# One stage of a two-block transformer kernel: the last two steps of a layer norm move to GpSimd, and three queues are reordered around them

## The chip, the cores and the metric

The kernel is one program on one core of a Trainium2 chip. The engines are TensorE (PE in the rows: matrix products and transposes; PEld: its weight loads), VectorE (DVE), ScalarE (ACT), GpSimd (POOL) and SyncE (SP), which here only issues DMAs. Each has a queue of its own, which it works in order; they meet at semaphores. The metric is the time of one execution on the device, in microseconds, as a median over runs; lower is better.

## The reference, cut to what matters

The program computes two transformer blocks on 2048 tokens of width 1024 in float32. The second block ends in a mixture of experts. The part that the change touches is what lies between attention and experts:

```
o   = concat(rmsnorm(o_mla), rmsnorm(o_gqa))           # halves of 512
h1  = layer_norm(ALPHA * h0 + o @ w_o, ln1_g, ln1_b)   # 1024 wide
logits = h1 @ w_router + b_router                      # 32 experts
top 4 experts and their softmax gates for each token
tables: for each expert the list of its tokens, then h1 gathered by expert
layer_norm(x, g, b) = (x - mean) / sqrt(var + 1e-5) * g + b
```

The experts then read h1 from DRAM (`h1d`), and their sums are added into a second copy (`sumd`).

## The kernel before, in words

The program is a chain of seven stages with a meeting of all engines between them: the mixer of the first block, its output product and norms (the *join* stage, tiles `j_...`), projections, attention, the *route* stage (tiles `o_...`), the experts (`e_...`), and a closing norm (`c_...`). The change is in the route stage alone, from about 2680 to 2975 us of the span.

The route stage works in 16 blocks of 128 tokens. Its loops run over i = 0 to 17, and each engine has an order of its own, written out by hand in `route_pe`, `route_act`, `route_dve`, `route_pool` and `route_sync`. The lists `b`, `a`, `v` and (after the change) `g` in `route_stage` repeat these orders; they give the semaphore values and the PSUM bank of each product (a ring of eight banks). No scheduler takes part.

In turn i the work is this.

- TensorE (`route_pe`): first half of the output product of block i (`project(i, 0)`, 24 matmuls, L2012), eight transposes of the attention output of block i+1 (`turn_o`, L1999), second half of the product (`project(i, 1)`); in its middle eight transposes of h1 of block i-1 (`turn_h`, L2021). Then the count of tokens per expert for block i-2 (`count`, L2035 and L2036) and the router product of block i-1 (`router`, L2028), which waits until ScalarE has copied the transposed h1 out of PSUM.
- ScalarE (`route_act`): rounds the transposed attention output (L2086), copies the transposed h1 into `hT` (L2103), takes the root of block i's variance (`lsd`, L2106), then the squares and the root for the RMS norm of block i+2 (L2077, L2079), then the exponentials of block i-1 (L2112). Roots and exponentials need different tables; a load of a table (ACT_TABLE_LOAD) stands between them.
- VectorE (`route_dve`): residual sum of each half (`residual`, L2149), low parts of the attention output (L2141), statistics of block i (`spread`, L2154 to L2156), `place(i-2)` (L2170 to L2176: where each token of block i-2 goes in the expert tables), `norm(i)` (L2161, and two products over 128x1024, L2165 and L2166, that give h1), `norms(i+2)` (the RMS norm of the attention output of block i+2: L2131, and L2134 twice), and `choose(i-1)` (L2181 to L2194: the top four experts of block i-1).
- GpSimd (`route_pool`): after loading constants, four scattering DMAs for each block (L2289) once `place` has written its slots. After the last it fetches the first table and gathers the first rows for the experts.
- SyncE (`route_sync`): loads of `od` and `h0d`, and for each block two stores of h1 once it is finished.

"T" is used below for the moment at which TensorE ends `project(i, 1)` and goes on to `count(i-2)`, the start of row L2035.

Of the kernel before, what the change touches and what calls it, by code (L numbers as in the profile page):

```python
# [1863 lines left out]
def route_stage(nc, A, banks, h0d, od, h1d, sumd, tabd, R, W, ident, eps_ln, eps_rms, since, ctx):  # L1864
# [25 lines left out]
    P.idf = sb("idf", [128, 16, 4])  # L1890
    sb("even", [128, 96])
    P.oTh = sb("oTh", [128, 2, 8, 128], F32R)
# [30 lines left out]
    for i in range(18):  # L1923
        now, nxt, back, far = i < 16, i + 1 < 16, 1 <= i < 17, i >= 2
        b += [("pj", i, 0)] if now else []
        b += [("to", i + 1, 0), ("to", i + 1, 1)] if nxt else []
        b += [("pj", i, 1)] if now else []
        b += [("th", i - 1, 0), ("th", i - 1, 1)] if back else []
        b += [("C", i - 2)] if far else []
        b += [("lg", i - 1)] if back else []  # L1930
        a += [("toh", i + 1, 0), ("toh", i + 1, 1)] if nxt else []
        a += [("th", i - 1, 0), ("th", i - 1, 1)] if back else []
        a += [("lsd", i)] if now else []
        a += [("sq", i + 2, 0), ("sq", i + 2, 1), ("sd", i + 2)] if i + 2 < 16 else []
        a += [("exp", i - 1)] if back else []
        v += [("pj", i, 0)] if now else []
        v += [("to", i + 1, 0), ("to", i + 1, 1)] if nxt else []
        v += [("pj", i, 1), ("st0", i), ("st1", i), ("ag", i)] if now else []
        v += [("C", i - 2), ("Macc", i - 2), ("pr", i - 2), ("pos", i - 2), ("sf", i - 2), ("slot", i - 2)] if far else []
        v += [("rs", i), ("ts", i), ("add", i)] if now else []  # L1940
        v += [("rms", i + 2), ("o", i + 2, 0), ("o", i + 2, 1)] if i + 2 < 16 else []
        v += [(n, i - 1) for n in ("lg", "m8", "i8", "idf", "ex", "neg", "oh", "M", "rec", "gate")] if back else []
    b += [("cnt",), ("tab",)]
    v += [("end", k) for k in range(34)]
# [9 lines left out]
def route_sync(nc, P):  # L1954
# [16 lines left out]
    for i in range(16):  # L1971
        if i + 2 < 16:
            load(i + 2)
        if i == 4:
            sp.wait_ge(*v.at("wo", 7))
            for c in range(2):
                sp.dma_start(P.R.raw[:, c].rearrange("p k n -> p (k n)"), A["wgu"][0, c]).then_inc(P.R.raw_full[c], 16)
        sp.wait_ge(*v.at("add", i))
        for d in (P.h1d, P.sumd):
            sp.dma_start(d[i * 128:(i + 1) * 128, :], P.h1[:, i % 3]).then_inc(*P.h1st[i % 3].more())  # L1980
# [4 lines left out]
def route_pe(nc, P):  # L1985
# [16 lines left out]
    def project(i, n):  # L2002
        p, f = opened("pj", i, n)
        if n == 0:
            pe.wait_ge(*v.at("to", i, 1))
        for k in range(8):
            if n == 1 and k == 4 and i >= 1:
                turn_h(i - 1)
            if i == 0 and n == 0:
                pe.wait_ge(*v.at("wo", k))  # L2010
            for m, (x, y) in enumerate(((P.oTh, P.woh), (P.oTh, P.wol), (P.oTl, P.woh))):
                t = pe.matmul(p[:, :], x[:, i % 2, k, :], y[:, k, n * 512:(n + 1) * 512],  # L2012
                              start=(k == 0 and m == 0), stop=(k == 7 and m == 2))
        t.then_inc(f, 1)

    def turn_h(i):
        pe.wait_ge(*v.at("add", i))
        for hf in range(2):
# [3 lines left out]
            t.then_inc(f, 1)  # L2022

    def router(i):
        p, f = opened("lg", i)
# [13 lines left out]
    for i in range(18):  # L2039
# [4 lines left out]
        if i < 16:  # L2044
            project(i, 1)
        if i == 16:
            turn_h(i - 1)
        if i >= 2:
# [66 lines left out]
def route_dve(nc, P):  # L2115
# [34 lines left out]

    def spread(i):
        x, s = P.hb[:, i % 3], P.sl_
# [3 lines left out]
        dve.bn_aggr(s[:, 12:14], s[:, 0:12]).then_inc(*v.step("ag", i))  # L2156

    def norm(i):
        x, y, s = P.hb[:, i % 3], P.h1[:, i % 3], P.sl_
        dve.wait_ge(*a.at("lsd", i))  # L2160
        link(dve.reciprocal(s[:, 15:16], s[:, 14:15]), "rs", i)  # L2161
        if i >= 3:
            dve.wait_ge(P.h1st[i % 3].sem, 32 * (i // 3))
            dve.wait_ge(*filled(P, ("th", i - 3, 1)))
        link(dve.scalar_tensor_tensor(out=y, in0=x, scalar=s[:, 12:13], in1=P.LN[:, 0, :], op0=ALU.subtract, op1=ALU.mult), "ts", i)  # L2165
        dve.scalar_tensor_tensor(out=y, in0=y, scalar=s[:, 15:16], in1=P.LN[:, 1, :], op0=ALU.mult, op1=ALU.add).then_inc(*v.step("add", i))  # L2166

# [46 lines left out]
    for i in range(18):  # L2214
# [4 lines left out]
        if i < 16:  # L2219
            residual(i, 1)  # L2220
            spread(i)
        if i >= 2:
            place(i - 2)
        if i < 16:
            norm(i)
        if i + 2 < 16:
            norms(i + 2)
        if 1 <= i < 17:
            choose(i - 1)
# [43 lines left out]
def route_pool(nc, P):  # L2273
# [10 lines left out]
    pool.wait_ge(P.const.sem, P.const.n)  # L2284
    pool.wait_ge(P.tab0.sem, P.tab0.n)
    for i in range(16):
        pool.wait_ge(*v.at("slot", i))
        for k in range(4):
            pool.indirect_dma_start(out=P.tabd, out_offset=bass.IndirectOffsetOnAxis(ap=P.slot[:, i, k:k + 1], axis=0),  # L2289
                                    in_=P.pair[:, i, k, :], in_offset=None).then_inc(*P.scat.more())  # L2290
    pool.wait_ge(P.scat.sem, P.scat.n)
# [849 lines left out]
```

## Time and profile before

| | us |
|---|---|
| median of 3 runs (lowest, highest) | 5685.53 (5682.82, 5690.87) |
| the profiled execution: its own time | 5690.87 |
| its span | 5689.7 |
| TensorE busy in the span | 5349.9 (94%) |
| VectorE busy | 3580.1 (63%) |
| ScalarE busy | 2682.3 (47%) |
| GpSimd busy | 744.9 (13%) |

The span is the time between the first and the last recorded instruction; the execution's own time is 1.2 us longer. The page of the profile gives the whole program; the route stage is about 5% of it, so it is read by windows and timelines. In a row of the timeline, a bracket says how long the engine was idle before the instruction and what it was waiting for; "issue" is a gap with no releaser in the records. Rows of several like instructions in succession are merged (x8), and the duration is from the first start to the last end.

### The profile page before, as it was taken

How to read it: one execution, taken by the hardware profiler on the slowest of the kernel's cores; microseconds unless marked ns; L12 is line 12 of the kernel's file. 1: busy time of each engine (PE TensorE's matmuls, PEld its weight loads, DVE VectorE, ACT ScalarE, POOL GpSimd, SP SyncE). 2: the span in 40 equal slices, each digit the busy share in tenths (PEclk: the TensorE clock that was granted, in tenths of full speed). 3: DMA queues.
4: the chain of work that ended last, by engine and by line, in shares of the span. 5: the costliest groups of instructions: out<-in, count | busy, mean ns of one | idle time of the engine just before them, and what ended most of it. 6: DMA issues, size and time to landing. Idle time of an engine off the chain costs nothing. (4 is left out here: it accounts for less than half of the span.)

```text
span 5689.7 us, 92463 instructions
## 1 busy us (share of the span) xinstructions
PE 5349.9 (94%) x30192; PEld 4771.6 (84%) x30193; DVE 3580.1 (63%) x6815; ACT 2682.3 (47%) x5312; POOL 744.9 (13%) x579
## 2 busy tenths in 40 slices
PE   8999979789799999998979999999999999999993
PEld 7777768678699999998768999999898888888883
DVE  6667757433466667776664755655667745477777
ACT  3444321333355556665333634543546534366664
POOL 1101125333100000000220100110101101010103
PEclk9999989899899999999989999999999999999997
DMA  3333234344510111201633744554557635477666
GB/s 142 115 115 101 92 124 167 113 130 138 171 59 28 39 53 38 74 33 51 161 105 114 249 151 153 197 169 155 194 188 234 232 127 169 136 230 247 240 226 229
DMA packets 260437, 809.25 MB, mean 142 GB/s; under 512 B 22304, under 2 KB 168448, under 8 KB 224512
## 3 DMA queue, kind: packets, MB, share of 16 engines
q1 hardware_dynamic: 230352, 717.05, 36.5%
q0 software_dynamic: 27536, 84.88, 6.8%
q10 hardware_dynamic: 2336, 4.45, 0.2%
q8 instruction: 136, 2.23, 0.2%
q14 instruction: 77, 0.63, 0.0%
HBM read 662.84 MB, written 143.47 MB: 142 GB/s over the span
## 5 line engine op out<-in xcount | busy, mean ns | idle before, releaser
L2726 DVE TENSOR_TENSOR e_wl<-r_raw,e_wh 128x1024 fp32r<-128x1024 f32 x770 | 930.6, 1223 | 480.0 <-DVEq L2354 479.3
L2575 PE MATMUL ps<-e_hT,e_wl 128*128 128x192 f32 (+5 forms) x4096 | 1196.6, 292 | 0.0
L2642 ACT CAST e_wh<-r_raw 128x1024 fp32r (+1 forms) x770 | 790.5, 1043 | 848.7 <-ACTq L2354 815.8
L2568 PE MATMUL ps<-e_hT,e_wh 128*128 128x384 f32 (+2 forms) x2560 | 797.6, 374 | 20.7 <-PEq L2354 20.3
L2575 PEld LDWEIGHTS ps<-e_hT,e_wl 128*128 128x128 f32 x4096 | 776.3, 190 | 10.7
L2570 PE MATMUL ps<-e_hT,e_wh 128*128 128x352 f32 (+2 forms) x1536 | 529.2, 345 | 9.0 <-PEq L2354 9.0
L2568 PEld LDWEIGHTS ps<-e_hT,e_wh 128*128 128x128 f32 x2560 | 480.4, 188 | 67.3 <-issue 27.2
L2574 PE MATMUL ps<-e_hT,e_wh 128*128 128x352 f32 (+2 forms) x1536 | 527.2, 343 | 0.0
L2596 PE MATMUL ps<-e_wh,e_aTh 128*128 128x512 f32 x1248 | 504.4, 404 | 5.0 <-PEq L2354 4.7
L1788 ACT CAST a_PT<-ps 128x512 fp32r<-128x512 f32 x512 | 288.0, 588 | 467.7 <-PE ps L1728 467.7
L1743 PE MATMUL ps<-a_PT,a_V 128*128 128x256 f32 (+1 forms) x3264 | 504.4, 294 | 0.2 <-DVE a_PT L1828 0.2
L1828 DVE TENSOR_TENSOR a_PT<-ps,a_PT 128x512 fp32r<-128x512 f32 (+1 forms) x640 | 377.6, 607 | 175.9 <-ACT a_PT L1788 158.4
L2596 PE MATMUL ps<-e_wh,e_aTl 128*128 128x512 f32 x1248 | 487.9, 391 | 0.0
L2596 PE MATMUL ps<-e_wl,e_aTh 128*128 128x512 f32 x1248 | 486.2, 390 | 0.0
L1815 DVE TENSOR_REDUCE a_sc<-ps 128x1 f32<-128x416 f32 (+1 forms) x640 | 365.1, 588 | 158.1 <-PE ps L1720 130.3
L1720 PE MATMUL ps<-a_K,a_Q 128*128 128x416 f32 (+1 forms) x1920 | 437.3, 358 | 17.5 <-DMA a_KR<-kTd 14.4
L1743 PEld LDWEIGHTS ps<-a_PT,a_V 128*128 128x128 f32 (+1 forms) x3264 | 419.4, 189 | 14.9 <-issue 13.5
L1800 ACT ACTIVATE a_P<-ps,a_sc 128x416 f32<-128x416 f32 (+1 forms) x640 | 386.2, 604 | 0.0
L1720 PEld LDWEIGHTS ps<-a_K,a_Q 128*128 128x128 f32 x1920 | 352.9, 190 | 30.9 <-issue 14.8
L386 PE MATMUL ps<-m_xh,m_wh 128*128 128x512 f32 x896 | 353.7, 395 | 5.3 <-DVE m_wl L671 5.3
L386 PE MATMUL ps<-m_xl,m_wh 128*128 128x512 f32 x896 | 349.7, 390 | 0.0
L386 PE MATMUL ps<-m_xh,m_wl 128*128 128x512 f32 x896 | 349.6, 390 | 0.0
(367 smaller groups left out, 9550.4 us busy)
## 6 DMA issues: line engine op xcount, KB each, us to landing
r_raw<-in_wgu SPq DMA_DIRECT2D x130, 2048.0 KB
r_raw<-in_wdn SPq DMA_DIRECT2D x64, 2048.0 KB
m_raw<-in_w SPq DMA_DIRECT2D x56, 1024.0 KB, 4.9
qTd<-p_qt SPq DMA_DIRECT2D x32, 640.0 KB, 6.6
e_bd<-in_bdn SPq DMA_DIRECT2D x32, 512.0 KB, 3.8
kTd<-p_kt SPq DMA_DIRECT2D x32, 448.0 KB, 3.7
a_Q<-qTd SPq DMA_DIRECT2D x7, 2048.0 KB, 9.4
a_V<-vd SPq DMA_DIRECT2D x24, 512.0 KB, 4.2
```

Of the source, the lines that this page charges most:

```text
L386: t = pe.matmul(p[:, :], x[:, w, i, j * 128:(j + 1) * 128], y[:, c % 2, i, :], start=(n == 0), stop=(n == 23))
L1720: t = pe.matmul(p[:, 0:w], x, y, start=(n == 0), stop=(n == len(todo) - 1))
L1743: t = pe.matmul(ps[b][:, 256 * half:256 * half + 256], P.V[0:r, j, x, :], P.PT[0:r, G % 2, y, j, :], start=(j == k == 0), stop=(j == NT - ...
L1800: act.activation(P.P[:, n % 2, lo:lo + w], p[:, 0:w], ACT.Exp, bias=P.sc[:, n % 2, 6:7], scale=SQK_M if P.steps[n][0] < 4 else SQK_G, accu ...
L1828: dve.tensor_tensor(lo, src, hi.bitcast(F32), ALU.subtract).then_inc(*v.step("t", n, c))
L2568: t = pe.matmul(both, wh, E.hT[:, :, k, 0:v], start=(k == 0), stop=False)
L2570: t = pe.matmul(p[:, 0:v], wh, E.hT[:, 0, k, 0:v], start=(k == 0), stop=False)
L2574: pe.matmul(p[:, 0:v], wh, E.hT[:, 1, k, 0:v], start=False, stop=False)
L2575: t = pe.matmul(p[:, 0:v], wl, E.hT[:, 0, k, 0:v], start=False, stop=(k == 7))
L2596: t = pe.matmul(E.G[g][:, :], x[:, 4 * h + k, b * 128:(b + 1) * 128], y[:, h, k * 512:(k + 1) * 512], start=(h == k == m == 0), stop=(h == ...
L2642: act.copy(E.wh[:, h, x], raw[:, 2048 * h + 1024 * i:2048 * h + 1024 * i + 1024]).then_inc(E.hi_full, 1)
L2726: return dve.tensor_tensor(lo, src, hi.bitcast(F32), ALU.subtract)
```

## The change

Four things are done in the route stage.

1. The layer norm of block i on VectorE is now one instruction, `tensor_scalar` with two column operands: (x - mean) * (1/sd), over 128x1024. The product with the gain and the sum with the bias are two `tensor_tensor` instructions of GpSimd over 128x1024, each waiting for the one before it. Whoever waited for the finished h1 (`turn_h`, the two stores) now waits for GpSimd.
2. On VectorE the norm follows the statistics directly, then come `norms(i+2)`, and `place(i-2)` is after both.
3. On TensorE the eight transposes of h1 leave the middle of `project(i, 1)`. They stand after `count(i-2)`, directly ahead of the router product of the same block.
4. GpSimd's scatters for block i-2 are now issued in turn i, behind the two products of block i; one unused tile of 384 bytes for each partition is dropped.

```diff
@@ route_stage
-    sb("even", [128, 96])
...
         b += [("pj", i, 1)] if now else []
-        b += [("th", i - 1, 0), ("th", i - 1, 1)] if back else []
         b += [("C", i - 2)] if far else []
-        b += [("lg", i - 1)] if back else []
+        b += [("th", i - 1, 0), ("th", i - 1, 1), ("lg", i - 1)] if back else []
...
@@ route_sync
-        sp.wait_ge(*v.at("add", i))
+        sp.wait_ge(*P.g.at("add", i))
         for d in (P.h1d, P.sumd):
@@ route_pe
         for k in range(8):
-            if n == 1 and k == 4 and i >= 1:
-                turn_h(i - 1)
...
-    def turn_h(i):
-        pe.wait_ge(*v.at("add", i))
+    def router(i):
+        pe.wait_ge(*g.at("add", i))
         for hf in range(2):
             p, f = opened("th", i, hf)
             for k in range(4):
                 t = pe.transpose(p[:, k * 128:(k + 1) * 128], P.h1[:, i % 3, (4 * hf + k) * 128:(4 * hf + k + 1) * 128], ident[:])
             t.then_inc(f, 1)
-
-    def router(i):
         p, f = opened("lg", i)
         pe.wait_ge(*a.at("th", i, 1))
...
             project(i, 1)
-        if i == 16:
-            turn_h(i - 1)
         if i >= 2:
             count(i - 2)
@@ route_dve
-    def spread(i):
+    def norm(i):
...
-        link(dve.scalar_tensor_tensor(out=y, in0=x, scalar=s[:, 12:13], in1=P.LN[:, 0, :], op0=ALU.subtract, op1=ALU.mult), "ts", i)
-        dve.scalar_tensor_tensor(out=y, in0=y, scalar=s[:, 15:16], in1=P.LN[:, 1, :], op0=ALU.mult, op1=ALU.add).then_inc(*v.step("add", i))
+        dve.tensor_scalar(P.h1[:, i % 3], x, s[:, 12:13], s[:, 15:16], ALU.subtract, ALU.mult).then_inc(*v.step("ts", i))
...
             residual(i, 1)
-            spread(i)
-        if i >= 2:
-            place(i - 2)
-        if i < 16:
             norm(i)
         if i + 2 < 16:
             norms(i + 2)
+        if i >= 2:
+            place(i - 2)
         if 1 <= i < 17:
             choose(i - 1)
@@ route_pool
-    pool.wait_ge(P.tab0.sem, P.tab0.n)
-    for i in range(16):
-        pool.wait_ge(*v.at("slot", i))
...
+    for i in range(18):
+        if i < 16:
+            x = P.h1[:, i % 3]
+            pool.wait_ge(*v.at("ts", i))
+            pool.tensor_tensor(x, x, P.LN[:, 0, :], ALU.mult).then_inc(*g.step("mul", i))
+            pool.wait_ge(*g.at("mul", i))
+            pool.tensor_tensor(x, x, P.LN[:, 1, :], ALU.add).then_inc(*g.step("add", i))
+        if i >= 2:
+            pool.wait_ge(*v.at("slot", i - 2))
...
```

VectorE's queue from the statistics of a block on; before (`o_sl` holds statistics, `o_h` is h1, `o_st` and `o_ob` belong to the RMS norm of block i+2, `o_C` to `o_slot` to `place`):

```order
L2156 BN_AGGR o_sl<-o_sl 128x2
L2170 COPY o_C<-ps 128x32
L2171 TENSOR_TENSOR o_Macc<-o_Macc,o_M 128x32
L2172 TENSOR_TENSOR o_pr<-o_oh,o_C 128x128
L2173 TENSOR_REDUCE o_pos<-o_pr 128x4
L2174 SCALAR_TENSOR_TENSOR o_sf<-o_idf,o_pos 128x4
L2176 CAST o_slot<-o_sf 128x4
L2161 RECIPROCAL o_sl<-o_sl 128x1
L2165 SCALAR_TENSOR_TENSOR o_h<-o_hb,o_sl,o_LN 128x1024
L2166 SCALAR_TENSOR_TENSOR o_h<-o_h,o_sl,o_LN 128x1024
L2131 RECIPROCAL o_st<-o_st 128x2
L2134 SCALAR_TENSOR_TENSOR o_ob<-o_ob,o_st,o_go 128x512 x2
```

The same stretch of VectorE's queue after the change:

```order
L2148 BN_AGGR o_sl<-o_sl 128x2
L2150 RECIPROCAL o_sl<-o_sl 128x1
L2154 TENSOR_SCALAR o_h<-o_hb,o_sl 128x1024
L2123 RECIPROCAL o_st<-o_st 128x2
L2126 SCALAR_TENSOR_TENSOR o_ob<-o_ob,o_st,o_go 128x512 x2
L2158 COPY o_C<-ps 128x32
L2159 TENSOR_TENSOR o_Macc<-o_Macc,o_M 128x32
L2160 TENSOR_TENSOR o_pr<-o_oh,o_C 128x128
L2161 TENSOR_REDUCE o_pos<-o_pr 128x4
L2162 SCALAR_TENSOR_TENSOR o_sf<-o_idf,o_pos 128x4
L2164 CAST o_slot<-o_sf 128x4
```

The six instructions of `place` stood between the statistics and the reciprocal that needs ScalarE's root; now nothing stands there, and the products `o_ob` come right behind the one instruction that is left of the norm.

TensorE's queue at the end of `project(i, 1)`, before (the transposes of `o_h` are twelve matmuls earlier, in the product's middle):

```order
L2012 MATMUL ps<-o_wol,o_oTh 128x512
L2012 MATMUL ps<-o_woh,o_oTl 128x512
L2035 MATMUL ps<-o_M,o_before 128x32
L2036 MATMUL ps<-o_Macc,o_ones 128x32
L2028 MATMUL ps<-o_wr,o_hT 128x32 x8
L2012 MATMUL ps<-o_woh,o_oTh 128x512
```

TensorE's queue at the same place after:

```order
L2008 MATMUL ps<-o_wol,o_oTh 128x512
L2008 MATMUL ps<-o_woh,o_oTl 128x512
L2029 MATMUL ps<-o_M,o_before 128x32
L2030 MATMUL ps<-o_Macc,o_ones 128x32
L2017 MATMUL ps<-ident,o_h 128x128 x8
L2022 MATMUL ps<-o_wr,o_hT 128x32 x8
L2008 MATMUL ps<-o_woh,o_oTh 128x512
```

Between the transposes of `o_h` and the router product that reads their copies (`o_hT`) there were twelve matmuls and the count; now there is nothing.

TensorE's queue at the end of the stage, before, from the count of block 13 on:

```order
L2035 MATMUL ps<-o_M,o_before 128x32
L2036 MATMUL ps<-o_Macc,o_ones 128x32
L2028 MATMUL ps<-o_wr,o_hT 128x32 x8
L2021 MATMUL ps<-ident,o_h 128x128 x8
L2035 MATMUL ps<-o_M,o_before 128x32
L2036 MATMUL ps<-o_Macc,o_ones 128x32
L2028 MATMUL ps<-o_wr,o_hT 128x32 x8
```

The same after the change:

```order
L2029 MATMUL ps<-o_M,o_before 128x32
L2030 MATMUL ps<-o_Macc,o_ones 128x32
L2017 MATMUL ps<-ident,o_h 128x128 x8
L2022 MATMUL ps<-o_wr,o_hT 128x32 x8
L2029 MATMUL ps<-o_M,o_before 128x32
L2030 MATMUL ps<-o_Macc,o_ones 128x32
L2017 MATMUL ps<-ident,o_h 128x128 x8
L2022 MATMUL ps<-o_wr,o_hT 128x32 x8
```

The last transposes of h1 (block 15) stood ahead of the count of block 14 and now stand behind it.

## Rows read from the trace of the kernel before

**Rows 1.** Windows (header: busy us, instructions by engine, granted clock, DMA) of three stretches.
```profile
2715.00:2720.00 5.00, 4.52 (x29) 3.97 (x29) 2.31 (x4) 1.27 (x3) 0.00 (x0) 1.00 1.01 339
...
2795.00:2800.00 5.00, 4.95 (x19) 4.13 (x20) 4.00 (x14) 1.35 (x4) 0.00 (x0) 0.66 0.98 170
...
2850.00:2900.00 50.00, 48.99 (x280) 41.66 (x278) 37.41 (x97) 21.20 (x44) 12.07 (x12) 1.00 0.47 128
```

**Rows 2.** Timeline of TensorE around block 8: start, us, engine, line, operation; brackets: idle before.
```profile
2827.69 1.09 PE L1999 MATMUL ps<-ident,o_ob 128*128 128x128 f32 x8 [0.34 <-issue]
...
2831.39 1.04 PE L2021 MATMUL ps<-ident,o_h 128*128 128x128 f32 x8
...
2835.00 0.30 PE L2035 MATMUL ps<-o_M,o_before 128*128 128x32 f32 x2
...
2835.36 1.95 PE L2028 MATMUL ps<-o_wr,o_hT 128*128 128x32 f32 x16
...
2843.21 1.09 PE L1999 MATMUL ps<-ident,o_ob 128*128 128x128 f32 x8 [0.34 <-issue]
```

**Rows 3.** Timeline of ScalarE and VectorE, block 8.
```profile
2832.02 1.07 ACT L2103 COPY o_hT<-ps 128x512 f32<-128x512 f32 x2 [1.77 <-PE ps L2021]
...
2833.11 1.28 ACT L2106 ACT_TABLE_LOAD   x1
...
2835.20 0.69 DVE L2149 SCALAR_TENSOR_TENSOR o_hb<-o_hb,ps 128x512 f32<-128x512 f32 x1 [3.19 <-PE ps L2012]
...
2837.24 0.21 DVE L2156 BATCH_NORM_AGGREGATE o_sl<-o_sl 128x2 f32<-128x12 f32 x1
...
2837.48 0.29 ACT L2106 ACTIVATE o_sl<-o_sl,junk 128x1 f32<-128x1 f32 x1 [3.09 <-DVE o_sl L2156]
...
2839.01 1.30 DVE L2165 SCALAR_TENSOR_TENSOR o_h<-o_hb,o_sl,o_LN 128x1024 f32<-128x1024 f32 x1
...
2839.18 0.30 ACT L2079 ACTIVATE o_st<-o_st,junk 128x2 f32<-128x2 f32 x1
...
2841.74 1.41 DVE L2134 SCALAR_TENSOR_TENSOR o_ob<-o_ob,o_st,o_go 128x512 f32<-128x512 f32 x2
```

**Rows 4.** Tile view, first stage and closing norm: VectorE, ns min/median/max, first and last start.
```profile
L991 DVE TENSOR_TENSOR j_yl<-j_yr,j_yh x32: 818/824/3024, 769.5 to 982.8; 128x640 fp32r<-128x640 f32 x32
...
L2933 DVE SCALAR_TENSOR_TENSOR c_st<-c_st x16: 159/966/2298, 5626.4 to 5680.0; 128x1 f32<-128x1 f32 x16
```

**Rows 5.** Timeline of the first residual stage, VectorE and GpSimd.
```profile
805.43 0.81 DVE L1009 TENSOR_SCALAR j_x<-j_x,j_st 128x1024 f32<-128x1024 f32 x1
...
806.16 3.69 DVE L991 TENSOR_TENSOR j_yl<-j_yr,j_yh 128x640 fp32r<-128x640 f32 x2
...
806.33 2.85 POOL L1051 TENSOR_TENSOR j_x<-j_x,j_LN 128x1024 f32<-128x1024 f32 x1 [4.65 <-DVE j_x L1009]
```

**Rows 6.** Timeline of the closing norm, GpSimd and VectorE.
```profile
5646.56 2.34 POOL L2947 TENSOR_TENSOR c_o<-c_o,c_LN 128x1024 f32<-128x1024 f32 x1 [1.37 <-ACT c_o L2909]
...
5647.96 0.97 DVE L2933 SCALAR_TENSOR_TENSOR c_st<-c_st 128x1 f32<-128x1 f32 x1
```

**Rows 7.** Timeline of block 5, in which a load lands late.
```profile
2783.86 0.30 PE L2035 MATMUL ps<-o_M,o_before 128*128 128x32 f32 x2
...
2791.54 0.63 ACT L2077 ACTIVATE o_sq<-o_ob 128x512 f32<-128x512 f32 x1 [4.90 <-DMA o_ob<-od]
...
2795.05 1.28 PE L1999 MATMUL ps<-ident,o_ob 128*128 128x128 f32 x8 [3.31 <-DVE o_ob L2134]
```

**Rows 8.** Timeline of the stage's end, TensorE.
```profile
2942.18 0.30 PE L2035 MATMUL ps<-o_M,o_before 128*128 128x32 f32 x2
...
2948.87 1.97 PE L2021 MATMUL ps<-ident,o_h 128*128 128x128 f32 x8 [4.38 <-DVE o_h L2166]
...
2950.92 0.60 PE L2035 MATMUL ps<-o_M,o_before 128*128 128x32 f32 x2
...
2951.76 3.60 PE L2028 MATMUL ps<-o_wr,o_hT 128*128 128x32 f32 x16
```

More of the change, by code:

```diff
@@ L1937, in route_stage @@
         v += [("to", i + 1, 0), ("to", i + 1, 1)] if nxt else []
-        v += [("pj", i, 1), ("st0", i), ("st1", i), ("ag", i)] if now else []
+        v += [("pj", i, 1), ("st0", i), ("st1", i), ("ag", i), ("rs", i), ("ts", i)] if now else []
+        v += [("rms", i + 2), ("o", i + 2, 0), ("o", i + 2, 1)] if i + 2 < 16 else []
         v += [("C", i - 2), ("Macc", i - 2), ("pr", i - 2), ("pos", i - 2), ("sf", i - 2), ("slot", i - 2)] if far else []
-        v += [("rs", i), ("ts", i), ("add", i)] if now else []
-        v += [("rms", i + 2), ("o", i + 2, 0), ("o", i + 2, 1)] if i + 2 < 16 else []
         v += [(n, i - 1) for n in ("lg", "m8", "i8", "idf", "ex", "neg", "oh", "M", "rec", "gate")] if back else []
+        g += [("mul", i), ("add", i)] if now else []
     b += [("cnt",), ("tab",)]
@@ L2156, in spread @@
         dve.bn_aggr(s[:, 12:14], s[:, 0:12]).then_inc(*v.step("ag", i))
-    def norm(i):
-        x, y, s = P.hb[:, i % 3], P.h1[:, i % 3], P.sl_
         dve.wait_ge(*a.at("lsd", i))
@@ L2284, in route_pool @@
     pool.wait_ge(P.const.sem, P.const.n)
-    pool.wait_ge(P.tab0.sem, P.tab0.n)
-    for i in range(16):
-        pool.wait_ge(*v.at("slot", i))
-        for k in range(4):
-            pool.indirect_dma_start(out=P.tabd, out_offset=bass.IndirectOffsetOnAxis(ap=P.slot[:, i, k:k + 1], axis=0),
-                                    in_=P.pair[:, i, k, :], in_offset=None).then_inc(*P.scat.more())
+    for i in range(18):
[7 more added lines that the diff above has]
+            pool.wait_ge(*v.at("slot", i - 2))
+            if i == 2:
+                pool.wait_ge(P.tab0.sem, P.tab0.n)
+            for k in range(4):
+                pool.indirect_dma_start(out=P.tabd, out_offset=bass.IndirectOffsetOnAxis(ap=P.slot[:, i - 2, k:k + 1], axis=0),
+                                        in_=P.pair[:, i - 2, k, :], in_offset=None).then_inc(*P.scat.more())
     pool.wait_ge(P.scat.sem, P.scat.n)
```

## Prediction, made before the changed kernel was run

> **What bounds the kernel now.** I read the page first: TensorE is busy 94% of the span, and the route stage, where every edit lies, is some 295 us of 5690. So only that stage's length can move. Next the windows of the stage: in 50 us of its steady part TensorE is busy for 48.99 at full granted clock, VectorE for 37.41, ScalarE for 21.20 and GpSimd for 12.07 [rows 1]. TensorE is the bound, and what can be won there is small. Next the timeline of one block [rows 2]: the transposes of the attention output start at 2827.69 and 2843.21, a period of 15.52 us. Ahead of them is a gap of 0.34 us without a named releaser. VectorE's two products `o_ob` run from 2841.74 to 2843.15 [rows 3], and the transposes that read them start at 2843.21: TensorE waits for VectorE there, briefly, in each block. In one block (block 5) it waits 3.31 us, because a load landed late [rows 7].
>
> So two chains run at nearly one length: TensorE's own queue, and the chain from T (here 2835.00) over residual, statistics, `place`, norm and `o_ob`, 8.15 us long (2843.15 - 2835.00), against 7.87 us of TensorE's own work up to the same place (2843.21 - 0.34 - 2835.00).
>
> **The change part by part.** All times are from T of a block; a block's rows are [rows 2, 3].
>
> *Transposes of h1 behind the product.* They take 1.04 us wherever they stand. Before, ScalarE's two copies of them (from 0.63 us after the transposes' start, 1.07 us long) lay beside twelve matmuls. Now the router product waits for them. Count 0.36 us, transposes from T+0.36, copies T+0.99 to T+2.06, router product at T+2.15 instead of T+1.40: 0.75 us of idle TensorE in each block. The router's 1.95 us and the next block's first half (7.87 - 0.36 - 1.95 = 5.56) follow: TensorE reaches the next transposes of `o_ob` at T+9.66. From there to the next T were 7.31 us (2835.00 - 2827.69), now 6.27 without the transposes. If nothing else made it wait the period would be 15.93, 0.41 more than now.
>
> *The norm directly behind the statistics.* The root of the variance came at T+2.48 (2837.48), straight after the statistics; the table load ahead of it ran from 2833.11, behind ScalarE's copies, well before T. Now the copies end at T+2.06, the table load takes T+2.08 to T+3.36, the root T+3.36 to T+3.65. `place`, which hid this wait, is behind. The reciprocal comes at T+3.68 and the new `tensor_scalar` at T+3.88. Its price is in the join stage, same form: 0.81 us [rows 5]; two products of about 1.3 us [rows 3] go away. It ends at T+4.69.
>
> *The RMS norm of block i+2.* ScalarE's squares and root end 2.0 us after the variance's root started (2839.18 + 0.30 - 2837.48), now at T+5.36. Alone VectorE would run `o_ob` from T+5.58 to T+7.0, well before T+9.66. TensorE's small wait would be gone.
>
> *GpSimd's two products.* They are of a kind that the join stage and the closing norm show: 2.34 us when nothing is in the way [rows 6], 2.85 when something is [rows 5]. What is in the way is VectorE. In the join stage a pair of `tensor_tensor` with both inputs in SBUF normally takes 0.82 us each, but there is one of 3.02 [rows 4], and the pair beside GpSimd's product lasts 3.69 instead of about 1.6 [rows 5]: GpSimd, which started 0.17 us later, is lengthened by 0.5 while the first runs, and the second is held until GpSimd ends. In the closing norm a VectorE instruction over a single column with two inputs in SBUF takes 0.97 us at the median instead of 0.16 [rows 4], and ends at 5648.93, 0.03 us behind GpSimd's product (5646.56 + 2.34) [rows 6]. So whoever starts first keeps the other out for its whole instruction, and they take turns.
>
> By that, GpSimd's first product runs from T+4.78 to T+7.13. VectorE's first `o_ob` is ready at T+5.58 and is held until T+7.13, runs to T+7.8; GpSimd's second, waiting since T+7.2, gets T+7.8 to T+10.15; VectorE's second `o_ob` gets T+10.15 to T+10.8. TensorE, there at T+9.66, starts at T+10.85 and waits 1.2 us. The period is 10.85 + 6.27 = 17.12, 1.60 more than now.
>
> The Trainium skill (SBUF — State Buffer, "Who interferes with whom") states this rule: VectorE with two SBUF inputs and a GpSimd instruction that reads SBUF contend for a shared pair of ports, and the second to start is blocked for the whole instruction, not slowed in proportion. The trace agrees, with 0.97 us where 0.16 is usual. A proportional sharing of the port would price the same overlap at far less than the 2.4 us for which the second `o_ob` is held.
>
> What lies behind: `place` (1.45 us, between 2837.36 and 2838.8 [rows 3]) and `choose` come later, but the count needs them only at the next T. VectorE's busy time falls from 37.41 / 50 x 15.52 = 11.6 to 9.8 us; with its waits (1.2 for the variance's root, 0.7 for the RMS root, 1.55 and 2.4 for the port) it comes to about 16.6, inside 17.12. GpSimd has 4.7 us of products and 5 us of scatters. SyncE stores h1 some 3 us later and so issues the next load later; the block is longer too, and some 10 us are left for a landing. I cost this at nothing; without that cover each late microsecond would be a wait of the same length.
>
> *The sum.* Thirteen ordinary blocks at +1.60: +20.8. The first two, at T of blocks 0 and 1, have no table load, yet come out within 0.2 us of it each.
> *Block 5*: the load lands at T+7.68 (2791.54 - 2783.86) and the transposes wait until T+11.19, then run partly at a granted clock of 0.66 [rows 1, 7], a loss of 3.0 + 1.7 = 4.7 us against an ordinary block. With the load at the same place after T, `o_ob` would be through at about T+11.4, when both products of GpSimd are over; TensorE would wait 1.7 us, and a wait of 1.6 us elsewhere left the clock full (2715 to 2720, granted 1.00) [rows 1]. The period is 17.7 instead of 20.1: -2.4.
> *Block 14*, without a next transpose: +0.8.
> *The end.* Before, the last transposes of h1 started 6.69 us after T (2948.87 - 2942.18), the count of block 14 at +8.74, the router product from +9.58 [rows 8]. Now VectorE has `place(13)` beside GpSimd's products: its second instruction is held until T+7.3, its third until T+9.7, `place` ends at T+10.75. `choose(14)` needs 2.1 us to the counts' operand (2950.92 less about 2948.8, when h1 was through and VectorE free), so the count is at T+12.95, the transposes from T+13.8 (1.97 long at the low clock), the copy of their second half ends at T+16.35, the router product starts at T+16.45: +6.9. Everything behind it, GpSimd's last scatters too, hangs on this.
> Sum: 20.8 - 2.4 + 0.8 + 6.9 = +26.1 us. The profiled execution took 5690.87 and so would take 5717.0; the median was 5685.53, and 5.3 us lower I forecast 5711.6.
>
> Costs that the trace of before does not show, bounded from both sides: how the port is handed over inside a pair of `o_ob` (nearest rows: the pair in the join stage, held 2.0 us; lower end: VectorE keeps it for both, 0), 0 to 2.4 us a block, I take 2.4, since the nearest row shows just such a pair divided; the clock under two short waits a block (nearest rows: 1.6 us of waiting at 1.00, 3.3 us followed by 0.66), 0 to 1.6 us a block, I take 0; the exposed copies, 0 to 0.8 us, I take 0.75. The smaller SBUF allocation: 0.
>
> **The rivals.**
> *A, the forecast,* +19 to +34: ports in turns. Chance 0.60.
> *B, VectorE keeps the port for both `o_ob`.* TensorE then waits only for the copies: 13 x 0.41 - 2.4 + 0.8 + 6.9 = +10.6, 5696. For it: the two `o_ob` follow each other without a semaphore between. Against it: so did the pair in the join stage, with its wait long met. 0.13.
> *C, no hold worth naming,* because the instructions meet at other moments than I place them. Steady part as in B; at the end `place` and `choose` run freely, and the router is late only by GpSimd's two products and the copies, about 2.7: +6.4, 5692. 0.11.
> *D, the clock falls too.* The waits of 0.75 and 1.2 us in each block, 10 us apart, bring the clock down as 3.3 us did. At 1.6 us a block for 13 blocks: +47, 5733. Against it: the full clock after the wait of 1.6 us. 0.09.
> *E, faster.* The wait for `o_ob` is what makes the period now; with `o_ob` ahead of `place` and 1.8 us less work on VectorE it goes away, block 5 loses its 3 us and its slow clock, and the copies are overlapped by TensorE's weight loads. 12 blocks at -0.4, block 5 at -4.7, +2.7 at the end: -7, 5679. It decides if the router's wait costs under about 0.1 us a block and `o_ob` is through before T+9. Against it: the router's first matmul reads what the last copy writes. 0.07.
>
> **How the numbers follow.** The forecast is A's, 5711.6. About 0.2% (11.4 us) is what a measurement of this kernel can tell from no change. Slower by more: most of A, D and a little of B, 0.70. Within: C, most of B, half of E, 0.24. Faster by more: 0.06. The range reaches down over B and C to 5691 and up to 5723, short of most of D.
>
> **What would show it.** In the changed profile's steady blocks: an idle of about 0.75 us ahead of the router product, released by ScalarE's copy; about 1.2 us ahead of the transposes of `o_ob`, released by VectorE; the pair `o_ob` at about 4.5 to 5 us from first start to last end where it was 1.41, its maximum single duration above 2 us; GpSimd's second product above 2.34; a period near 17.1; the norm's `tensor_scalar` at 0.81; the last router product some 16.4 us after the last T. A period near 15.9 with `o_ob` through by T+8.5 would make me wrong by B or C; a granted clock below 1.00 in the steady part would speak for D.

## The result and the profile after

The changed kernel took 5714.49 us (median of 4 runs, 5711.43 to 5719.85) against 5687.57 for the kernel before in the same comparison: a ratio of 1.0054, 95% interval 1.0040 to 1.0068. By the medians that is +26.9 us (the interval of the ratio, taken over all rounds, stands for 23 to 39 us); the forecast was +26.1 (5711.6) and the range 5691 to 5723. A second comparison (a2 below) gave 5722.46 against 5689.85, 1.0063 (1.0049 to 1.0076).

Windows of the changed kernel, over the stretches of [rows 1] (columns as there):

```profile
2715.00:2720.00 5.00, 4.06 (x15) 3.46 (x16) 2.86 (x4) 1.17 (x2) 0.34 (x1) 0.66 0.77 272
...
2795.00:2800.00 5.00, 5.00 (x30) 4.34 (x30) 3.18 (x4) 3.94 (x8) 2.76 (x2) 1.00 0.05 15
...
2850.00:2900.00 50.00, 45.18 (x247) 37.47 (x246) 40.20 (x86) 19.30 (x40) 25.84 (x18) 1.00 0.37 127
```

In 50 us of the steady part TensorE is busy for 45.18 where it was 48.99, still at a granted clock of 1.00. GpSimd is busy for twice its former time. VectorE is *longer* busy than before (40.20 for 37.41) though it has less work: time in which an instruction is held counts as busy, as the pair `o_ob` below shows. The stretch from 2715 us now has a clock of 0.66 instead of 1.00, and that from 2795 us 1.00 instead of 0.66.

TensorE's timeline, the rows that answer to [rows 2]:

```profile
2854.47 1.09 PE L1997 MATMUL ps<-ident,o_ob 128*128 128x128 f32 x8 [0.79 <-DVE o_ob L2126]
...
2860.98 0.31 PE L2029 MATMUL ps<-o_M,o_before 128*128 128x32 f32 x2
...
2861.34 1.07 PE L2017 MATMUL ps<-ident,o_h 128*128 128x128 f32 x8
...
2863.23 1.94 PE L2022 MATMUL ps<-o_wr,o_hT 128*128 128x32 f32 x16 [0.82 <-DVE o_sl L2147]
...
2871.63 1.09 PE L1997 MATMUL ps<-ident,o_ob 128*128 128x128 f32 x8 [0.79 <-DVE o_ob L2126]
```

The period is 17.16 us (2871.63 - 2854.47), from 15.52. There are two waits: 0.82 us ahead of the router product, which needs ScalarE's copies (the profile names a VectorE statistic there, which had ended just then; the wait in the code is for the copies), and 0.79 us ahead of the transposes of `o_ob`.

ScalarE, VectorE and GpSimd in the same block, answering to [rows 3]:

```profile
2862.02 1.07 ACT L2095 COPY o_hT<-ps 128x512 f32<-128x512 f32 x2 [3.42 <-PE ps L2017]
...
2863.11 1.28 ACT L2098 ACT_TABLE_LOAD   x1
...
2864.40 0.30 ACT L2098 ACTIVATE o_sl<-o_sl,junk 128x1 f32<-128x1 f32 x1
...
2864.93 0.81 DVE L2154 TENSOR_SCALAR o_h<-o_hb,o_sl 128x1024 f32<-128x1024 f32 x1
...
2865.83 2.40 POOL L2275 TENSOR_TENSOR o_h<-o_h,o_LN 128x1024 f32<-128x1024 f32 x1 [4.91 <-DVE o_h L2154]
...
2866.10 0.30 ACT L2071 ACTIVATE o_st<-o_st,junk 128x2 f32<-128x2 f32 x1
...
2866.63 4.95 DVE L2126 SCALAR_TENSOR_TENSOR o_ob<-o_ob,o_st,o_go 128x512 f32<-128x512 f32 x2
...
2868.30 2.72 POOL L2277 TENSOR_TENSOR o_h<-o_h,o_LN 128x1024 f32<-128x1024 f32 x1
```

The table load now stands behind the copies, and the root comes at 2864.40, 3.4 us after T, not 2.5. The `tensor_scalar` takes 0.81 us. Then the two engines alternate: GpSimd's first product ends at 2868.23; the pair `o_ob`, begun at 2866.63, lasts 4.95 us instead of 1.41; GpSimd's second product is lengthened to 2.72 by the first half of that pair, and the second half runs behind it. TensorE starts 0.05 us after the pair's end.

The end of the stage, answering to [rows 8]:

```profile
2962.08 0.30 PE L2029 MATMUL ps<-o_M,o_before 128*128 128x32 f32 x2
...
2966.97 2.33 DVE L2159 TENSOR_TENSOR o_Macc<-o_Macc,o_M 128x32 f32<-128x32 f32 x1
...
2969.34 2.49 POOL L2277 TENSOR_TENSOR o_h<-o_h,o_LN 128x1024 f32<-128x1024 f32 x1
...
2969.99 1.86 DVE L2162 SCALAR_TENSOR_TENSOR o_sf<-o_idf,o_pos 128x4 f32<-128x4 f32 x1
...
2974.32 0.61 PE L2029 MATMUL ps<-o_M,o_before 128*128 128x32 f32 x2 [7.75 <-DVE o_M L2179]
...
2975.16 1.95 PE L2017 MATMUL ps<-ident,o_h 128*128 128x128 f32 x8
...
2977.88 3.59 PE L2022 MATMUL ps<-o_wr,o_hT 128*128 128x32 f32 x16 [0.77 <-ACT o_hT L2095]
```

Two small instructions of `place(13)`, normally 0.19 and 0.16 us, take 2.33 and 1.86 beside GpSimd's products. The count of block 14 waits 7.75 us for `choose`, which is behind them; the last router product starts 15.80 us after T, where it was 9.58. The hold is the smaller part of this: in e3 below, which only moves the transposes, it starts 12.3 us after T, and in e2, which has all three orders but no product on GpSimd, 13.9.

### The profile page after: what moved, and what is told of

The parts are those of the page before. It is cut to its first block and busy times, and to the rows that moved or that the text cites. A ratio compares the mean times of both kernels' runs of the same rounds, so it can differ in the third digit from the quotient of the medians.

```text
span 5712.3 us, 92480 instructions
## 1 busy us (share of the span) xinstructions
PE 5356.1 (94%) x30192; PEld 4774.5 (84%) x30193; DVE 3610.4 (63%) x6799; ACT 2686.0 (47%) x5312; POOL 829.6 (15%) x611
## 5 line engine op out<-in xcount | busy, mean ns | idle before, releaser
L2562 PE MATMUL ps<-e_hT,e_wh 128*128 128x384 f32 (+2 forms) x2560 | 798.9, 375 | 19.5 <-PEq L2348 18.2
L1720 PE MATMUL ps<-a_K,a_Q 128*128 128x416 f32 (+1 forms) x1920 | 436.2, 357 | 17.5 <-DMA a_KR<-kTd 14.3
```

The lines of the kernel that those rows point to most:

```text
L1720: t = pe.matmul(p[:, 0:w], x, y, start=(n == 0), stop=(n == len(todo) - 1))
L2562: t = pe.matmul(both, wh, E.hT[:, :, k, 0:v], start=(k == 0), stop=False)
```

## The experiments

Each ratio is against runs of the kernel before on the same chip. "Period" is from one count to the next in the steady part of the profiled execution; "clock" is the granted clock from 2800 to 2860 us. The ratio is taken over all rounds, the us column is the difference of the medians, so the two differ a little. The diffs below are shortened, and the comments in them are added here.

| run | change against its base | ratio (95%) | us | period | clock |
|---|---|---|---|---|---|
| changed kernel | | 1.0054 (1.0040, 1.0068) | +26.9 | 17.17 | 1.00 |
| a2 | the same again | 1.0063 (1.0049, 1.0076) | +32.6 | 17.16 | 1.00 |
| e1 | changed, transposes in the middle | 1.0044 (1.0030, 1.0058) | +29.3 | 17.07 | 1.00 |
| e2 | changed, norm on VectorE | 1.0051 (1.0038, 1.0065) | +31.9 | 17.5, each fourth 19.1 | 0.89 |
| e3 | before, transposes moved | 1.0044 (1.0030, 1.0058) | +27.2 | 17.5, each fourth 19.1 | 0.89 |
| e4 | before, VectorE's order | 0.9995 (0.9986, 1.0004) | -3.3 | 14.96 | 1.00 |
| e5 | changed, products later | 1.0068 (1.0054, 1.0082) | +34.9 | 16.2 to 19.7 | 0.89 |
| e6 | before, scratch products | 1.0152 (1.0136, 1.0167) | +86.5 | 20.8 to 22.3 | 0.89 |
| e7 | before, scratch memsets | 1.0006 (0.9997, 1.0015) | +4.1 | 15.51 | 1.00 |
| e8 | before, transposes moved, count behind them | 1.0032 (1.0021, 1.0044) | +19.7 | 17.15, later 15.56 | 0.91 |
| e9 | e2 with one more wait | 1.0058 (1.0044, 1.0072) | +33.8 | 17.3 | 1.00 |
| e10 | e6, products later | 1.0014 (1.0004, 1.0023) | +7.4 | 15.85 | 1.00 |
| e11 | e1 and e5 together | 1.0022 (1.0013, 1.0031) | +14.3 | 15.1 to 16.8, once 24.8 | 0.97 |

My theory was that VectorE and GpSimd keep each other out of a shared port, in turns, and that this sets the block; the rival was that the exposed copies (and the late root) cost it.

**e1, transposes of h1 back in the middle.**

```diff
+            if n == 1 and k == 4 and i >= 1:
+                turn_h(i - 1)          # waits for GpSimd's sum; gone from router()
```

> The changed kernel, with the transposes of h1 back in the middle of the second half of the product (they wait for GpSimd). Port theory (VectorE's two products o_ob and GpSimd's two products keep each other out in turns, and this sets the block): no copy is exposed and ScalarE's root is on time, so GpSimd's first product runs T+3.9 to T+6.2, o_ob ends at about T+10.0, then 7.31 us: a period of 17.3, no better than the changed kernel's 17.17; only the end of the stage is some 4 us shorter. In all +20 to +26 against before. Rival (the exposed copies are what costs): the period falls by 0.8 to 1.6 us a block, in all +8 to +16 against before.

Its timeline, one block:

```profile
2863.96 0.30 PE L2034 MATMUL ps<-o_M,o_before 128*128 128x32 f32 x2
...
2868.67 4.92 DVE L2133 SCALAR_TENSOR_TENSOR o_ob<-o_ob,o_st,o_go 128x512 f32<-128x512 f32 x2
...
2873.65 1.09 PE L1998 MATMUL ps<-ident,o_ob 128*128 128x128 f32 x8 [1.71 <-DVE o_ob L2133]
...
2881.01 0.30 PE L2034 MATMUL ps<-o_M,o_before 128*128 128x32 f32 x2
```

The wait ahead of the router product is gone, and the period stays (17.05 here): the pair still takes 4.92 us, and TensorE waits 1.71 us for it instead of 0.79, at a full clock. The rival falls as the sole cause: without exposed copies the port alone makes the same block. The total of +29.3 us is above the +20 to +26 that I had written, though its interval (17 to 33) includes them.

**e2, norm on VectorE; e3, only the transposes moved.** Both are built from the kernel before: e3 has TensorE's new order alone, e2 has VectorE's too. GpSimd only scatters in both.

```diff
-            if n == 1 and k == 4 and i >= 1:
-                turn_h(i - 1)
+    def router(i):                     # waits for v.at("add", i), the eight transposes, then the product
+        ...                            # e2 alone: also norm(i), norms(i + 2) ahead of place(i - 2), as in e4
```

> The changed kernel's three orders, but the two products of the norm stay on VectorE (2.6 us) and GpSimd only scatters. Port theory: nothing is held, o_ob is through at about T+8.0, the copies stay exposed (0.8 us), a period of 16.3, the end +4: +11 to +15 against before, some 13 less than the changed kernel. Rival (the order on VectorE and the late root cost it, not the port): the period stays near 17.2, about +25.

> The kernel before, with only the transposes of h1 moved behind the count, directly ahead of the router product. Own price of the exposed copies: 0.8 us a block over what TensorE waits now, so a period of 16.3 against 15.52, and +2.7 at the end: +11 to +14. Rival (it hides in the wait for o_ob that is there anyway): 0 to +4.

Both came out at twice the expected cost, so my price for the exposed copies was wrong. e2's total is even near its rival's +25, but not by the rival's cause: e3 leaves VectorE's order as it was and has the same periods, and TensorE has no wait for `o_ob` in the steady part of either, only the one ahead of the router product. Its row in e3, and then the windows behind it:

```profile
2845.52 1.94 PE L2023 MATMUL ps<-o_wr,o_hT 128*128 128x32 f32 x16 [0.82 <-DVE o_sl L2148]
```

```profile
2845.00:2847.00 2.00, 1.48 (x14) 1.51 (x14) 1.79 (x8) 1.97 (x4) 0.00 (x0) 1.00 0.03 8
...
2847.00:2849.00 2.00, 2.00 (x10) 1.66 (x10) 1.89 (x4) 1.92 (x6) 1.37 (x2) 0.65 0.01 1
...
2849.00:2851.00 2.00, 2.00 (x6) 1.55 (x5) 1.96 (x4) 0.99 (x1) 1.50 (x2) 0.50 0.16 58
...
2851.00:2853.00 2.00, 2.00 (x10) 1.65 (x9) 1.77 (x9) 0.31 (x2) 1.15 (x1) 1.00 1.06 395
```

TensorE is busy without a gap from 2847 on, but at a granted clock of 0.65 and then 0.50 (1.2 GHz) until about 2851, before it is back at 1.00 (2.4 GHz). In e3 nine matmuls start 0.43 us apart there instead of 0.23. With this order of TensorE, a full clock and no second wait, a block is 16.16 us long (two blocks of e5 below); here it is 17.5, and each fourth is 19.1. So the exposed copy costs 0.8 us of waiting, and in these two kernels 1.3 to 3.0 us of slow clock besides. The changed kernel's first steady block is of this kind (17.75 us at 0.90, and no second wait); its other eleven have the same wait of 0.82 us, a second of 0.79, and no such fall.

**e4, VectorE's order alone.**

```diff
             spread(i)
-        if i >= 2:
-            place(i - 2)
-        if i < 16:
             norm(i)
         if i + 2 < 16:
             norms(i + 2)
+        if i >= 2:
+            place(i - 2)
```

> The kernel before, with only VectorE's order changed: norm directly behind the statistics, then the RMS norm of block i+2, then place. Both theories: o_ob is through at T+7.2 instead of T+8.15, TensorE stops waiting for it, a period of 15.0 to 15.1 instead of 15.52: -3 to -7. If the small wait ahead of the transposes is TensorE's own, 0.

```profile
2800.00:2860.00 60.00, 60.00 (x338) 51.71 (x338) 48.05 (x122) 27.67 (x56) 15.31 (x16) 1.00 0.41 142
```

TensorE is busy for 60.00 of 60 us: 14.96 is its own length of a block, and the wait for `o_ob` cost 0.56 of 15.52. Over 12 blocks this is 6.7 us. The measured -3.3 us, with an interval from -8 to +2, can be told neither from that nor from nothing. It has the lowest time against the kernel before of all versions that I ran, and is not shown to beat it.

**e5, the same products, later.**

```diff
-            pool.wait_ge(*v.at("ts", i))
+            pool.wait_ge(*(v.at("o", i + 2, 1) if i + 2 < 16 else v.at("ts", i)))
```

> The changed kernel, with GpSimd's first product of block i waiting until both o_ob products of block i+2 are done; the same work, no meeting of the two. Port theory: TensorE no longer waits for o_ob, a period of 16.4 to 16.8 (the exposed copy stays, and place and choose are held instead, up to VectorE's full length): some 6 to 9 us less than the changed kernel, +16 to +21 against before. Rival (GpSimd's work costs by its length wherever it is): no change against the changed kernel, +25 or more.

The tile view of the pair (ns min/median/max of one):

```profile
L2126 DVE SCALAR_TENSOR_TENSOR o_ob<-o_ob,o_st,o_go x32: 744/748/753, 2684.5 to 2938.3; 128x512 f32<-128x512 f32 x32
```

Nothing holds `o_ob` any more, as the port theory has it, and the time did not fall: a miss for my number, and the total is the rival's. Its cause is not. In two of the twelve steady blocks the clock stays at 1.00, and they take 16.16 us, 1.0 less than in the changed kernel; in the other ten, with the same wait of 0.82 us ahead of the router product, it falls as in e2, and they take 17.7 to 19.7. What GpSimd's work costs by its length alone is tested in e10.

**e6 and e7, scratch work beside the kernel before.** Two more GpSimd instructions a block on a tile that nobody reads; in e6 `tensor_tensor`, in e7 `memset`.

```diff
+            pool.wait_ge(*v.at("ts", i))
+            pool.tensor_tensor(P.zrow[:], P.zrow[:], P.LN[:, 0, :], ALU.mult)   # e7: pool.memset(P.zrow[:], 1.0)
+            pool.tensor_tensor(P.zrow[:], P.zrow[:], P.LN[:, 1, :], ALU.add)    # e7: the same memset
```

> The kernel before, with two more GpSimd tensor_tensor over a scratch tile of 128x1024 in each block, started when the norm's first product is done; nobody waits for them but GpSimd's own scatters. Port theory: they push o_ob to about T+12.7, a period near 20.1 instead of 15.5, +45 to +60. Rival (no hold; GpSimd's results being late is what costs in the changed kernel): within 2 us of before.

> As the run with scratch products, but the two GpSimd instructions are memsets of the same tile, which read nothing. If only a GpSimd instruction that reads SBUF keeps VectorE's two-input instructions out: within 2 us of before, o_ob's pair at 1.41 us. If any GpSimd instruction does: +0.5 to +2 us a block, +6 to +25.

e6, one block:

```profile
2881.83 1.28 DVE L2167 SCALAR_TENSOR_TENSOR o_h<-o_h,o_sl,o_LN 128x1024 f32<-128x1024 f32 x1
...
2881.88 3.47 POOL L2292 TENSOR_TENSOR o_zrow<-o_zrow,o_LN 128x1024 f32<-128x1024 f32 x1 [9.43 <-DVE o_h L2166]
...
2883.23 5.41 DVE L2135 SCALAR_TENSOR_TENSOR o_ob<-o_ob,o_st,o_go 128x512 f32<-128x512 f32 x2
...
2885.43 2.67 POOL L2294 TENSOR_TENSOR o_zrow<-o_zrow,o_LN 128x1024 f32<-128x1024 f32 x1
...
2888.70 1.97 PE L2000 MATMUL ps<-ident,o_ob 128*128 128x128 f32 x8 [4.32 <-DVE o_ob L2135]
```

GpSimd's first product waits for VectorE's (1.28) and runs; the pair `o_ob` takes 5.41 us, and TensorE waits 4.32 us, though no result of GpSimd is needed. The +86.5 us are a miss upwards from +45 to +60. The hold is about as forecast: the transposes start 12.20 us after T (2888.70 - 2876.50), and by the 7.31 us from there to the next T the period would be 19.5. The rest of the 20.8 to 22.3 is the clock, which falls in each block (0.89), and which I had again left out; another 10 us come ahead of the stage's first count.

In e7 the pair is as ever:

```profile
L2135 DVE SCALAR_TENSOR_TENSOR o_ob<-o_ob,o_st,o_go x32: 744/749/754, 2681.3 to 2913.9; 128x512 f32<-128x512 f32 x32
```

The first memset (0.96 us) lies beside VectorE's second product of the norm, which takes 1.28 us as before, and the second beside the first half of the pair. Memsets only write, and these hold nothing; +4.1 us (interval -2 to +9) cannot be told from nothing. Both are as the Trainium skill has it (SBUF — State Buffer, "Who interferes with whom": GpSimd's reads contend with a VectorE instruction that has two SBUF inputs, its writes do not).

**e8, the count between the transposes and the router product.**

```diff
-            if n == 1 and k == 4 and i >= 1:
-                turn_h(i - 1)
...
-        if i == 16:
+        if 1 <= i < 17:
             turn_h(i - 1)
         if i >= 2:
             count(i - 2)
```

> The kernel before, with the transposes of h1 behind the product, and the count now between them and the router product, so that 0.36 us of the copies' 0.8 are covered. If the clock falls with the idle time that is left ahead of the router (0.82 us did it in each block of the run with only the transposes moved): with some 0.45 us left either the clock stays at 1.00 and the period is 15.9 to 16.0, in all +5 to +9, or it falls as there and the period is 17.1 or more, +20 or more.

```profile
2800.00:2860.00 60.00, 58.20 (x300) 49.20 (x298) 38.69 (x97) 23.39 (x47) 12.07 (x12) 0.91 0.47 123
```

The wait left is 0.45 us, and the clock falls all the same, in ten of twelve steady blocks: 17.15 us a block. In the last two it did not, with the same wait, and they took 15.55; the fall costs 1.6 us a block here. So the wait alone does not decide whether the clock falls.

**e9, e2 with a second wait and no more work.**

```diff
         pe.wait_ge(*v.at("o", i, 1))
+        if i >= 3:
+            pe.wait_ge(*v.at("ex", i - 3))
```

> The run with the norm on VectorE and the changed kernel's orders, in which the clock fell in each block (periods 17.5 and 19.1), with one more wait and no more work: the transposes of the attention output of a block wait for a later step of choose, some 0.8 us behind the point that TensorE has reached, as they wait for VectorE in the changed kernel. If this second wait is what leaves the clock of the changed kernel full: a period near 17.2 at a granted clock of 1.00, in all +20 to +25, less than that run. If GpSimd's products themselves have to do with it, or the length alone: periods of 18.2 and more at a clock below 0.95, +35 or more.

```profile
2740.00:2800.00 60.00, 55.07 (x287) 46.27 (x286) 42.60 (x113) 24.13 (x50) 13.63 (x15) 0.95 0.63 204
...
2800.00:2860.00 60.00, 53.23 (x296) 44.82 (x294) 39.67 (x97) 23.58 (x46) 13.42 (x14) 1.00 0.32 113
...
2860.00:2920.00 60.00, 55.06 (x286) 46.20 (x286) 42.63 (x109) 24.53 (x50) 12.47 (x13) 0.94 0.36 127
```

In seven blocks, the whole middle stretch among them, TensorE waits 0.82 us ahead of the router product and 1.0 to 1.24 us ahead of the transposes, and its clock is 1.00, at 17.14 to 17.34 us a block; in the other five it fell (0.90 in each, 17.5 us), and the second wait is missing. So GpSimd's products are not needed for a full clock. That the second wait is what keeps it up is not shown: in a block with a fall TensorE reaches the transposes 11.2 us after T, behind the 10.96 at which they start otherwise, so that the fall itself removes the wait; the first block at full clock (from 2770.32) follows one without a second wait, and the first that falls again (from 2891.50) follows one with it. The total is a miss: +33.8 us where this branch had +20 to +25. By total time e9 (1.0058) and e2 (1.0051) are not apart.

**e10, e6's products behind `o_ob`.**

```diff
-            pool.wait_ge(*v.at("ts", i))
+            pool.wait_ge(*(v.at("o", i + 2, 1) if i + 2 < 16 else v.at("add", i)))
```

> The kernel before with the same two scratch products of GpSimd as the run that took 79 us more in the stage, but started when o_ob of block i+2 is done. Port theory: they hold only parts of choose, which nobody waits for; a period of 15.5, within 5 us of before. Rival (GpSimd's work costs by its length): +40 or more.

The same GpSimd work costs 7.4 us (interval 2 to 13) instead of 86.5. VectorE is held in `choose`, is busy for 57 of 60 us, and TensorE waits 0.66 us for `o_ob`, hence 15.85 and not 15.5. What is held:

```profile
2834.31 2.38 POOL L2292 TENSOR_TENSOR o_zrow<-o_zrow,o_LN 128x1024 f32<-128x1024 f32 x1 [6.02 <-DVE o_ob L2135]
...
2834.88 1.83 DVE L2185 CAST o_idf<-o_i 128x4 f32<-128x4 uint32 x1
...
2836.77 2.40 POOL L2294 TENSOR_TENSOR o_zrow<-o_zrow,o_LN 128x1024 f32<-128x1024 f32 x1
...
2837.14 2.18 DVE L2188 TENSOR_TENSOR o_oh<-o_erow,o_idf 128x128 f32<-128x128 f32 x1
```

Of the two VectorE instructions the second has two inputs and takes 0.29 us otherwise. The first, a cast of 128x4 between two tiles in SBUF, has one input and takes 0.17 us otherwise, and it is held all the same, in 15 of 16 blocks. So "two inputs in SBUF", as I had put it, is not the whole of the condition.

**e11, both costs taken out.**

```diff
+            if n == 1 and k == 4 and i >= 1:
+                turn_h(i - 1)
...
-            pool.wait_ge(*v.at("ts", i))
+            pool.wait_ge(*(v.at("o", i + 2, 1) if i + 2 < 16 else v.at("ts", i)))
```

> The changed kernel with both of its costs taken out: transposes of h1 in the middle of the product, GpSimd's products behind o_ob. The norm's two products stay on GpSimd. No wait of TensorE is left in the steady part, VectorE's place and choose are held but end before the next T plus 0.9: a period of 14.96 as in the run with only VectorE's order changed, the end some +1 to +3: -6 to +1 against before. If place and choose, held by GpSimd, set the block instead: a period of 15.5 to 16.5, +3 to +15.

```profile
2862.42 2.37 POOL L2282 TENSOR_TENSOR o_h<-o_h,o_LN 128x1024 f32<-128x1024 f32 x1 [5.43 <-DVE o_ob L2133]
...
2862.46 2.37 DVE L2166 TENSOR_TENSOR o_Macc<-o_Macc,o_M 128x32 f32<-128x32 f32 x1
...
2864.86 2.40 POOL L2284 TENSOR_TENSOR o_h<-o_h,o_LN 128x1024 f32<-128x1024 f32 x1
...
2864.87 2.53 DVE L2167 TENSOR_TENSOR o_pr<-o_oh,o_C 128x128 f32<-128x128 f32 x1
...
2867.31 1.09 PE L2020 MATMUL ps<-ident,o_h 128*128 128x128 f32 x8 [0.26 <-POOL o_h L2284]
```

The second case. Two instructions of `place`, of 0.19 and 0.29 us, take 2.37 and 2.53 us, and VectorE comes late to the next block's residual and statistics (0.94 us after T in the block that begins at 2855.40, where it was 0.20 before). Everything behind follows: `o_ob`, GpSimd's products, and TensorE's transposes of h1, which wait for GpSimd's sum. The blocks take 15.8 us on average, and one late landing cost 9 us. It halves the loss and stays slower than before (1.0013 to 1.0031).

**a2, the changed kernel again.**

> The changed kernel itself once more, beside runs of before on one chip as the variants had. If the full clock in its steady part is a property of its pattern of waits and not of one execution: periods of 17.17 at a granted clock of 1.00 again, and +25 to +31 against before, about as much as the variant with the norm on VectorE (+29) in which the clock fell. If the first profile was a lucky one: periods of 17.5 and more at a clock near 0.9.

Periods of 17.16 at 1.00, in all twelve steady blocks. The full clock was no accident of one execution. The total, +32.6 us, is a little above the +25 to +31 that I had written.

## Why the prediction was right, and where not

*The steady block.* Forecast 17.12, measured 17.17. The pair was forecast at 5.2 us and took 4.95; the second wait was forecast at 1.2 and is 0.79. So the transposes of `o_ob` start 10.65 us after T, and not 10.85. A second error went the other way: I had taken the transposes of h1 as 1.04 us of TensorE's queue, from a row that merges eight and counts to the last one's end. The first matmul behind them starts 0.79 us after them in the trace of before, so the second half of the product keeps 6.51 of its 7.31 us, and not 6.27. The two errors are 0.2 us each and cancel, which is luck. From T of block 2 to T of block 14 (2737.31 to 2928.12 before, 2740.24 to 2946.81 after) twelve periods grew by 15.8 us, from 190.81 to 206.57; I had 11 x 1.6 - 2.4 = 15.2.

*Block 5.* I left its late load in place (17.7). In both profiles of the changed kernel it is an ordinary block of 17.17. Nor does the late landing come with the TensorE order of before: in e7, which has the same, that block took 15.92. The profiled execution of before, from which I worked, was the slowest of its runs.

*The first two blocks.* Forecast +3.2; from the stage's first transposes to the first count it is +6.3 (52.6 to 58.9). The wait for the first `o_ob` grew from 1.60 to 3.96 us, and the clock fell behind it (0.66 on average from 2715 to 2720). Of the 6.3 us, 2.4 are this longer wait and 2.5 lie between the transposes behind it and the first count. The other 1.4 come earlier, from a slow clock behind a wait of 2.94 us that both kernels have (granted 0.50 for 6.1 us behind that wait, until 2703.0; before it was 3.4 us); no run shows that they belong to the change. The first two blocks are the term that I mis-sized: I costed the clock at nothing everywhere.

*Block 14 and the end.* Forecast +0.8 and +6.9, measured +1.2 and +6.2. I had the second and third instruction of `place` held; it was the second and the fifth.

*The sum.* 6.3 + 15.8 + 1.2 + 6.2 = +29.5 us in the stage, against +26.1 forecast and +26.9 (in a2 +32.6) measured in total. Against a stage of before with an ordinary block 5, 4.6 us shorter, it would be some +34, an estimate from the same rows; how many executions of before have the late block is not known. The mechanism is shown, but that the total agrees to 0.8 us is luck: the first two blocks are off by 3.1 us, the other terms by less and in both directions, and the two comparisons are 6 us apart.

*Rival D.* It was wrong for this kernel and right for its neighbours: e2, e3, e5 and e8 lose 1.3 to 3.0 us in most blocks to the clock behind a wait of 0.45 to 0.82 us. My reason against it, a full clock after one wait of 1.6 us, was one row at one place. What follows from it is that the two costs of the change don't add as I had them add. Taking the port away (e2) or the exposed copies (e1) alone gives nothing back; the other, or the clock, fills the block. Rivals B and C fell with the alternation in the rows; E fell with the 0.82 us.

*Open.* Why the clock stays full with waits of 0.82 and 0.79 us (changed kernel), 0.82 and 1.24 (seven blocks of e9) or 1.71 alone (e1), and falls with 0.82 alone (e2, e3) or with 4.32 alone (e6), no run settles; in e5 and e8 the same wait goes with a fall in ten blocks and with none in two.

## What to carry to other kernels

Before moving elementwise work to GpSimd, look at what VectorE does in those microseconds: beside a GpSimd instruction that reads SBUF, one with two inputs in SBUF, however small, was held until GpSimd's ended, and one cast with a single input was too. The price is read off where the same pair of engines already meets in the trace. A transpose, a copy on another engine and a product of the copy want other TensorE work between them; its lack cost 0.8 us of waiting in a block here, and in some kernels more than that in clock. When two costs share one chain, an experiment that removes one of them may show nothing.

## What the runs showed of the hardware

- A VectorE `tensor_tensor` over 128x32 took 2.33 us instead of 0.19 beside a GpSimd product over 128x1024; the same scratch work of GpSimd, moved behind `o_ob`, cost 7 us in place of 87 (e10, e6).
- A VectorE cast of 128x4 with one input took 1.83 us instead of 0.17 beside such a product (e10). A `tensor_reduce` of 128x128 beside one took 0.28 us, as ever (changed kernel, 2969.67).
- GpSimd memsets of 128x1024 (0.96 us each) beside VectorE's second product of the norm and the first of `o_ob` held neither (1.28 us; 749 ns at the median, 754 at most).
- In e8, with one wait of 0.45 us a block ahead of the narrow products, the granted clock was 0.90 in ten steady blocks and 1.00 in the last two, with the same wait in all of them.
- In e9 the blocks with a fall of the clock lack the second wait: the fall makes TensorE late enough to remove it.
